# First attention: TensorE's order within a visit, and ScalarE's copy of the shares

## The reference, cut to what matters

```python
def sliding_window_sink_attention(h, positions, w_qkv, q_gain, k_gain, sinks, w_o):
    qkv = h @ w_qkv                      # 16 query heads, 2 key/value heads of 64
    q = partial_rope(rmsnorm(q, q_gain), positions)
    k = partial_rope(rmsnorm(k, k_gain), positions)
    ...
    def block_fn(i):                     # 4 blocks of 128 queries, 256 keys each
        s = jnp.einsum('bqkgd,bskd->bkgqs', qb, kb).astype(jnp.float32) * scale
        s = jnp.where(valid, s, -jnp.inf)
        p = jax.nn.softmax(jnp.concatenate([s, sink_col], axis=-1), axis=-1)[..., :-1]
        o = jnp.einsum('bkgqs,bskd->bqkgd', p.astype(vb.dtype), vb)
    ...
    return out @ w_o
```

## Time and profile before

| what | value |
|---|---|
| median of 3 runs | 2261.47 us (2260.85 to 2262.05) |
| profiled execution | 2259.29 us, of which the span is 2257.5 us |
| TensorE busy | 2226.1 us, 99% of the span |
| VectorE busy | 1190.2 us, 53% |
| ScalarE busy | 892.9 us, 40% |
| DMA | 258.76 MB, mean 115 GB/s |

### The profile page before, as it was taken

The page is one execution under the profiler, slowest core; times in us unless marked ns, Lnnn a source line. Parts: engine busy times, 40 slices in busy tenths (PEclk is TensorE's granted clock), DMA queues, the critical chain, the costliest instruction groups (busy, mean ns, idle before and its releaser), DMA issues. The chain is left out here.

```text
span 2257.5 us, 26396 instructions
## 1 busy us (share of the span) xinstructions
PE 2226.1 (99%) x10712; PEld 1787.3 (79%) x10712; DVE 1190.2 (53%) x1603; ACT 892.9 (40%) x1413; POOL 165.3 (7%) x147
## 2 busy tenths in 40 slices
PE   8999999999999999999999999999999999999998
PEld 6766888888777778888888878887788888888886
DVE  4775756543465753333337446567742447553453
ACT  4664322223354533322334236467742324332331
POOL 2112000000000010000001002023210001000001
PEclk9999999999999999999999999999999999999999
DMA  9432565632222123322223324323332232332222
GB/s 334 150 122 84 215 214 197 216 110 95 92 66 66 57 68 103 103 93 95 92 85 102 103 76 154 115 91 121 105 116 102 84 112 84 103 97 100 94 85 84
DMA packets 82169, 258.76 MB, mean 115 GB/s; under 512 B 8800, under 2 KB 17376, under 8 KB 82048
## 3 DMA queue, kind: packets, MB, share of 16 engines
q1 hardware_dynamic: 82048, 257.07, 33.7%
HBM read 252.78 MB, written 4.26 MB: 114 GB/s over the span
## 5 line engine op out<-in xcount | busy, mean ns | idle before, releaser
L876 PE MATMUL pb<-hhi,whi 128*128 128x512 f32 x1936 | 766.5, 396 | 2.0 <-ACT hhi L1318 2.0
L878 PE MATMUL pb<-hhi,wlo 128*128 128x512 f32 x1936 | 754.3, 390 | 2.7 <-DVE wlo L1589 2.7
L880 PE MATMUL pb<-hlo,whi 128*128 128x512 f32 x1936 | 754.8, 390 | 0.0
L1589 DVE TENSOR_TENSOR wlo<-raw,whi 128x1024 fp32r<-128x1024 f32 x360 | 446.2, 1244 | 546.6 <-ACT whi L1280 546.5
L1280 ACT ACTIVATE whi<-raw 128x1024 fp32r<-128x1024 f32 x360 | 378.9, 1056 | 694.0 <-PE pb L880 672.1
L876 PEld LDWEIGHTS pb<-hhi,whi 128*128 128x128 f32 x1936 | 363.5, 188 | 88.6 <-issue 16.0
L878 PEld LDWEIGHTS pb<-hhi,wlo 128*128 128x128 f32 x1936 | 363.7, 188 | 79.1 <-DVE wlo L1589 4.1
L880 PEld LDWEIGHTS pb<-hlo,whi 128*128 128x128 f32 x1936 | 363.3, 188 | 78.0 <-DVE hlo L1686 1.3
L876 PE MATMUL pb<-ahi,whi 128*128 128x512 f32 x848 | 334.0, 394 | 1.6 <-ACT ahi L1476 0.9
L878 PE MATMUL pb<-ahi,wlo 128*128 128x512 f32 x848 | 330.2, 389 | 1.1 <-DVE wlo L1589 1.1
L880 PE MATMUL pb<-alo,whi 128*128 128x512 f32 x848 | 330.5, 390 | 0.0
(11 more groups left out here) (263 smaller groups left out, 1721.3 us busy)
## 6 DMA issues: line engine op xcount, KB each, us to landing
raw<-stream SPq DMA_DIRECT2D x360, 512.0 KB, 3.3
slab<-ada_w SPq DMA_DIRECT2D x80, 512.0 KB, 5.1
early<-ada_w SPq DMA_DIRECT2D x32, 256.0 KB, 8.0
slab<-sums SPq DMA_DIRECT2D x32, 256.0 KB, 4.1
X<-xT SPq DMA_DIRECT2D x8, 256.0 KB, 5.0
ya<-slab SPq DMA_DIRECT2D x8, 256.0 KB, 3.4
slab<-ya SPq DMA_DIRECT2D x8, 256.0 KB, 5.1
outT<-X SPq DMA_DIRECT2D x8, 256.0 KB, 2.1
```

What stands on the lines that cost most here:

```text
L876: e.matmul(out, wh, hi, start=s.k == 0, stop=False)
L878: e.matmul(out, wl, hi, start=False, stop=False)
L880: i = e.matmul(out, wh, lo, start=False, stop=s.last)
L1589: e.tensor_tensor(wlo[:, u % NW, :], raw[:, u % NRAW, :], whi[:, u % NW, :].bitcast(F), ALU.subtract).then_inc(*v_cut.up(u))
```

## The change

In `advance`, which writes the ticks of one visit, the order was exps (stage 1), scores (stage 0), turned (stage 2), values (stage 3). Now it is share, turns, exps, scores, turned, values. "share" and "turns" are new names for parts of stages 3 and 2. TensorE does the transposes of the weights at "turns" and nothing at "turned"; the other engines do their part at "turned" and nothing at "turns". The transposes of the share stand in "share" on TensorE, and ScalarE's copy of them stands in "share" too. VectorE's list is the same as before.

```diff
         def advance():
-            for stage in (1, 0, 2, 3):
-                for it in flying:
-                    if it[0] == stage:
-                        tick(("scores", "exps", "turned", "values")[stage], *it[1])
-                        done.add((stage, *it[1]))
+            at = {it[0]: it[1] for it in flying}
+            for name, stage in (("share", 3), ("turns", 2), ("exps", 1), ("scores", 0), ("turned", 2), ("values", 3)):
+                if stage in at:
+                    tick(name, *at[stage])
+                    done.add((stage, *at[stage]))
...
@@ TensorE
                 m.then_inc(*t_att.up(("o", t, i)))
             if pair:
                 give(("o", t), v_att, ("ot", t))
+
+        def share(t, pair):
+            if pair:
                 b = take(("share", t))
                 w.wait_ge(v_att, ("inv", t))
                 for i in range(4):
...
-              "krope": lambda: turn_halves("k"), "kspread": kspread, "vturn": vturn, "query": query, "scores": scores, "turned": turned,
+              "krope": lambda: turn_halves("k"), "kspread": kspread, "vturn": vturn, "query": query, "scores": scores, "turns": turned, "share": share,
...
@@ ScalarE
-        def values(t, pair):
+        def share(t, pair):
             if pair:
                 if t >= 2:
                     w.wait_ge(v_half, ("oa", t - 2))
                 w.wait_ge(t_att, ("share", t))
                 e.activation(OT[t % 2], bank(("share", t)), ACT.Copy).then_inc(*a_att.up(("share", t)))
+
+        def values(t, pair):
+            if pair:
                 w.wait_ge(v_att, ("ot", t))
                 e.activation(ahi[:, t, :], OT[t % 2], ACT.Copy).then_inc(*a_half.up(("oa", t)))
```

More of the change, by code:

```diff
@@ L1558, in scalar @@
         e.activation(condp.rearrange("p (k m) -> p k m", m=32)[:, 0:8, 0:1], W("c", 0, 8).unsqueeze(2), ACT.Silu).then_inc(*a_att.up("cond"))
-        do = {"unnormed": unnormed, "factor": factor, "cut": cut, "sq": sq, "norm": norm, "gnorm": gnorm, "rows": rows, "modrows": modrows, "sines": sines, "tables": tables, "evac": evac, "exps": exps, "turned": turned, "values": values,
+        do = {"unnormed": unnormed, "factor": factor, "cut": cut, "sq": sq, "norm": norm, "gnorm": gnorm, "rows": rows, "modrows": modrows, "sines": sines, "tables": tables, "evac": evac, "exps": exps, "turned": turned, "share": share, "values": values,
               "vturn": vturn, "start": start, "turn": turn, "gather": gather, "dtturn": dtturn, "gsq": gsq, "xsilu": xsilu, "bturn": bturn,
```

## The result

The changed kernel takes 2264.28 us, the median of 22 runs (2262.15 to 2267.05); the kernel before takes 2261.16 us on the same chip, also over 22 runs. The ratio is 1.0015, 95% interval [1.0009, 1.0021]: 3.1 us slower, with 2.0 to 4.7 by the interval. That is told apart from no change, but is less than the 0.2% at which the prediction draws its line. 2264.0 was forecast.

A forecast was written before the change was run, and what follows sets the result against it. The prediction took TensorE, busy 99% of the span, as the bound. Its terms, 0.2 - 1.3 + 2.5 - 0.9 + 1.9 + 0.1 + 0.1 = +2.6, taken as +2.5 on 2261.47, gave 2264.0 us, 8-in-10 range 2259.5 to 2267.3.

The forecast's parts named there:

- The banks' loop: Share visits beside w_o: scores wait 3.1 and 2.55 us for ScalarE to free the first transposed block's bank; +2.5 and +1.9.
- The other waits: TensorE's waits in the plain visits, for ahi and ahead of the products with w_o, each given its own size.
- The first plain visit: First plain visit beside w_o: waits of 2.07 us become one of 1 to 1.7; term -1.3 us.
- The second: Second plain visit beside w_o: the 1.10 us wait goes, one of about 0.3 comes; term -0.9 us.
- the third: Third plain visit beside w_o: values wait about 0.95 us for ScalarE's copy, where they waited 0.99; term +0.1 us.
- The product: Last three visits: the product that waited 0.9 us for ahi waits about as long; term +0.1 us.
- idle time: TensorE between 135 and 190 us: 8 to 9 us idle after the change, against 6.2 before.
- The lead-up: Attention up to 136 us: the share's transposes wait once for VectorE's spread inverse; +0.2 us, bounds 0 and 1.5.
- The sum: All terms of lead-up and visits beside w_o together: +2.6 us, taken as +2.5, giving 2264.0 us.
- Rival 3: The two long waits make TensorE's clock fall, adding 2 x 1.6 = 3.2 us: 2267.2 us; chance 0.05.
- Rival 1: ScalarE's loop is not closed and share visits lose their waits of 0.59 us: -3.7 us, 2257.8; chance 0.10.
- Rival 2: The delay spreads to all three plain visits' values and the lead-up's 1.5 us stays: +5.4 us, 2266.9; chance 0.17.

The follow-up runs named there:

- e_late_early: Changed kernel, with the exponentials one product behind their scores' visit on ScalarE, from item (5, 1) on only: 2257.94 us, ratio 0.9986 to the kernel before.
- e_fill3: Changed kernel, with three useless float32 products put into each share visit's long wait on TensorE: 2262.95 us, ratio 1.0007 to the kernel before.
- e_share: Kernel before, with only the share's transposes and their copy moved ahead; the weights' transposes stay behind the scores: 2259.36 us, ratio 0.9992.
- e_share_late_early: Kernel before, with only the share moved ahead, plus early exponentials in the dense part alone: 2257.43 us, ratio 0.9985.
- e_exps1st: Changed kernel, but ScalarE copies the share behind the exponentials instead of ahead: 2262.17 us, ratio 1.0004 to the kernel before.
- e_turns: Kernel before, with only the weights' transposes moved ahead of the scores; the share and its copy stay at the visit's end: 2263.03 us, ratio 1.0011.
- e_three_before: Kernel before, with three instead of four tiles of w_o open, so four banks go round: 2261.87 us, ratio 1.0005.
- e_three: Changed kernel, with three instead of four tiles of w_o open, so four banks go round: 2262.55 us, ratio 1.0008 to the kernel before.
- e_early: Changed kernel, with the exponentials one product behind their scores' visit on ScalarE everywhere: 2262.22 us, ratio 1.0001 to the kernel before.
- e_fill: Changed kernel, with 11 useless float32 products put into each share visit's long wait on TensorE: 2275.83 us, ratio 1.0065 to the kernel before.

## Why the prediction was right, and what of it was not

**The banks' loop: right, to a third of a microsecond.** It foretold waits of L1050 for ScalarE's copy of 3.1 and 2.55 us; they are 3.33 and 2.88. The working holds step by step in ScalarE's rows: copy, four exponentials (2.33 us against 2.34), sinks, copy. e_late_early shows that this list is the cause: with TensorE's order untouched and the exponentials moved, the slowdown turns into a gain. So it is not TensorE's order by itself.

**The other waits: right in kind.** The first plain visit waits 1.06 us for L1825 where 1 to 1.7 was said, and its waits of 2.07 us are gone. The second waits 0 (0.3 was said), the third 0.32 (0.95); with the clock held in e_fill3 they wait 0.40 and 1.36. The product waits 1.26 us for ahi, where I said about as long as the 0.90 before. Together the dense part waits 8.85 us (the five waits 1.06, 3.33, 2.88, 0.32, 1.26) for 6.24 before: **+2.6**, with idle time foretold as 8 to 9. The lead-up has two waits for L1880 where one was said, 0.25 us at 118 and 0.49 at 132, and lost 0.1 us; +0.2 was forecast.

**The sum: right, for a clock at 1.00.** e_fill3 has the changed kernel's order with the clock held, and its visits can be set beside those of the kernel before, each from its first row to the first product behind it. They come out at -1.4, +2.5, -0.9, +2.1 and +0.3 us; the forecast's terms were -1.3, +2.5, -0.9, +1.9 and +0.1. The rest of the dense part adds 0.1 us, as forecast. The dense part as a whole is 2.8 us longer than before (62.5 for 59.8), and the medians put e_fill3 1.4 us above the kernel before, with -0.5 to 3.6 by the interval.

**The clock: the step that failed.** Rival 3 was given 0.05, and the sum held nothing for it. It happened, at both long waits: the work was stretched by 2.6 and 1.6 us, where 1.6 each was worked out. The prediction had noted that none of the waits before was as long as these, and gave that too little weight. It had also tied the fall between 10 and 20 us to the wait of 3.9 us for a transfer. The rows don't bear this out. That wait ends at 3.90 us, from 10 to 15 us TensorE works at a clock of 1.00, and the clock falls at the products that stand behind a wait of 1.07 us:

```profile
10.00:15.00 5.00, 4.95 (x41) 1.00 1.07 378
15.00:20.00 5.00, 3.93 (x13) 0.68 1.08 366
```

```profile
16.50 3.99 PE L938 MATMUL pb<-early,slab 128*32 128x512 f32 x8 [1.07 <-DMA early<-ada_w]
```

Read so, the kernel before already showed that a wait of about 1 us can be followed by a fall. I had also taken it for something that the change alone could bring. The Trainium skill's rule ("TensorE: Matmul & The Clock Gate", "HAM oscillation — how this bites in real kernels"), that idle gaps can throw TensorE back to half its clock, is borne out here in kind: 0.59, 0.73 and 0.66 at waits of 3.33 and 2.88 us, and 1.00 when the gap was filled with products. In size it is not, for that page of the Trainium skill wants a longer gap than any of the waits that did it here; the measurement decides. The rule stood in the prediction and should have had a term in the sum.

**The work between the waits.** Without its waits and without the stretching by the clock, the dense part takes 59.8 - 6.2 = 53.5 us before and 65.3 - 8.85 - 4.2 = 52.3 after, 1.3 us less for the same instructions. e_late_early has 57.0 - 4.8 = 52.2, e_share 57.7 - 4.1 = 53.6, e_share_late_early 56.3 - 2.9 = 53.4: so it goes with the transposes' place. The eight transposes of the first plain visit take two times 0.66 us with a stop between the earlier trace rows and 1.04 in one go after. The prediction had used these sizes (0.66 and 1.05) in its visits. Whether the stops are all of it is not shown.

So in the profiles the balance is +0.1 (lead-up), +2.6 (waits), +4.2 (clock), -1.3 (work), together +5.6, where the clock's net share is 2.8. The last term is what the others leave of the difference found, so that the sum closes says nothing; that e_late_early has the same 52.2 does. The spans differ by 5.0, since the kernel before lost 0.5 us in its own fall at 590 us: TensorE's waits common to both profiles lie 5.65 us apart at 200 us and 5.15 apart at 804. The medians differ by 3.1 only: the profiled execution of the kernel before was 1.9 us under its median.

How much of the 3.1 us is the clock's can only be bounded. Every timed execution has its mean granted clock. The kernel before had 0.995 in 14 of its 87 executions in the calls of the experiments (mean time 2262.7 us), 0.996 in 32 (2261.7), 0.997 in 35 (2260.4) and 0.998 in 6 (2259.1), so it loses the clock in some and not in others. The 22 executions of the kernel after have 0.993 to 0.996. At an equal mean clock it is slower by 2.1 us (2264.8 in 9 executions for 2262.7 at 0.995, 2263.8 in 8 for 2261.7 at 0.996), which leaves 1 us of the 3.1. Its mean clock is lower by 0.0013, which is 2.9 us of 2260 if all of it is lost work. Both are estimates, from rounded values, across calls and with falls anywhere in the program; they put the clock's part at 1 to 3 us. So a forecast of 2264.0 that held nothing for the clock was met by a median of 2264.28, and the closeness is partly luck.

**Rivals 1 and 2.** Rival 1, that the loop is not closed, is out: two long waits. Rival 2, that the delay spreads over all visits, is out as well: of the plain visits only the third waits for ScalarE, 0.32 us, or 1.36 with the clock held. Its price of +5.4 us was nearly reached in the profiles, but by the clock.

## What to carry to other kernels

When a unit of work is moved ahead on one engine, look up for each buffer it now takes who gives it back, and what stands in that engine's list ahead of the giving back; here four exponentials (2.3 us) stood there, and moving them in ScalarE's list took 6.3 us off the changed kernel (in medians of two calls) and nothing off the one before, where TensorE waits for no bank from that list. Put a term for the clock into the sum wherever a change gathers small waits into one long one, take off the waits that a slower TensorE no longer meets, and keep in mind that the price varies from one execution to the next. And where two orders are changed at once, time the halves: here one half loses, the other does not, and their medians don't add up to the whole.

## What the runs showed of the hardware

- In the attention, the granted clock fell at single waits of TensorE of 3.33 us (after, e_exps1st), 3.28 (e_turns), 2.99 and 2.21 (e_three_before), 2.88 (after), 2.76 (e_three) and 2.04 (e_early). It stayed at 1.00 behind 2.36 (e_turns), 2.10 and 2.01 (both e_three), and behind waits of 1.74 us or less, but for one place: once it fell behind 0.43, 0.54 and 1.10 us close together, which in the profile of before left it alone.
- Elsewhere shorter waits were enough, in some executions. At a wait of 0.45 us near 590 us it fell in 3 of the 13 profiles (before, e_three_before, e_late_early), and at one of 0.39 us between 224 and 238 us in 4 (e_turns, e_early, e_three, e_fill); in the others it stayed at 1.00 there. So no length of a single wait parts the two cases.
- In the kernel after, the clock was at half for 6.8 us at the first long wait and for 3.4 us at the second. It stretched the work by 2.6 and 1.6 us.
- A plain float32 product of 128 x 512 takes TensorE 0.88 us (e_fill: 11 in 9.71, two records to a product), where a float32r one starts 0.23 us after the last (before, at a clock of 1.00).
